# Gathered expert rows in another order: the context's second tile takes two quarters in the first stretch, and x's first mixer starts three pairs later

## The chip, the cores and the metric

The kernel runs on one core of a Trainium2 chip. The metric is the device time of one execution in microseconds, as the median of several runs. TensorE is called PE in the profile, VectorE DVE, ScalarE ACT, GpSimd POOL and SyncE SP.

## What is computed

Two blocks of two layers each, for 256 tokens x and 256 context tokens, width 1024. The part that matters here is the first block. Each of its layers normalises and modulates the tokens, runs a token mixer (a gated linear recurrence with a short convolution), and then an expert layer:

```
qr = (h @ wq)                      # 8 heads, two halves of 128
scores = qr . subkeys              # 128 keys for each half
s1, i1 = top_k(scores[half 0], 16); s2, i2 = top_k(scores[half 1], 16)
top, pos = top_k(s1[:, None] + s2[None, :], 16)
eidx = i1 * 128 + i2 at pos;  gate = softmax(top)
out = sum over 128 chosen e of gate[e] * gelu(u[e] . h) * v[e]
```

Layer 0 does it for the context and for x, layer 1 for x alone. Each token thus takes 128 of 16384 rows of u and v, other rows for every token. The modulation vectors are products of a condition with `w_mod`, 24 MB a layer. The second block (differential attention, a convolution by spectra, two large MLPs) comes after and reads x.

## The kernel before

**Tiles and selections.** 256 tokens are two tiles t of 128 partitions. A selection is one chosen expert of every token of a tile: GpSimd gathers 128 rows of u and v together (8 KB each, 1 MB in all) by one indirect DMA into one of `SLOTS` = 6 buffers `uv` (L2419). VectorE takes the dot product of u with the token (`dot`, L2134), ScalarE the gelu (L1484), VectorE the weight (`weigh`, L2144 or L2146), and v is added by TensorE into a PSUM bank with a diagonal matrix (L1058) or by VectorE into `acc` (L2158). `on_pe` says which: odd selections go to TensorE, except in segments 3 and 6, and all of the first 24. A buffer comes free with its addition, so GpSimd can run six selections ahead.

**Segments and pairs.** `SEGS` lists segments (which, tile, from, to), where which is 0 for the context in layer 0, 1 for x in layer 0, 2 for x in layer 1. The selections of all segments are numbered through; two make a pair g. `PAIRS` holds each segment's last pair: 64, 80, 144, 208, 256, 320, 384. The first weave runs pairs 0 to 256, the second 256 to 384. At a segment's end `flush` (L2161 ff.) adds the sums into the tokens. The context's second tile is split: its first quarter is segment 1, and the other three are segment 4, after the two tiles of x.

**Picks.** A pick (which, tile, quarter) turns the scores of two heads into 32 indices and gates: some 60 VectorE instructions in five pieces (`pick`, L2020 ff., with `top16` at L2002 to L2017). `PICK_ORDER` is their order, `PICK_SLOTS` the pairs at which the five pieces are put in. x's scores use the same memory as the context's, so the context's scores for the later quarters are stored in DRAM (`held`, ScalarE's queue) and read back (`reload_piece`).

**The weave.** Each engine's program is written out by hand with the same function:

```python
for g in range(first, last + 1):
    segment(g, first, last)
    for n, x in enumerate(streams):
        while due[n] is not None and due[n] <= g:
            due[n] = next(x, None)
```

`segment` issues the dots of pair g and the weights and additions of pair g - 1; each stream is a generator that yields the pair at which its next piece is due. The engines run in order and meet at semaphores only. The streams of the first weave are, by pair number: the queries and scores of the context (`WQ[0]`, 0 to 8), four picks (0 to 12), the norm of x (4), its mixer in layer 0 (`TIMES[1]`: eight chunks of `w_in` from 10 on, sixteen scan levels to 34, tail at 35), its output product (`OUT`, 41), norm (`POST`, 46), queries (`WQ[1]`, 52 to 63), eight picks of x (58 to 97), three picks of the context (101 to 115), the modulations of layer 1 and of block two's first layer (`MOD_AT` 84 and 108: 12 chunks of 2 MB each, one every two pairs, TensorE at L833, VectorE's bias at L1730), the convolution filters (`FILTERS`, 136 to 154), and the norm and mixer of x in layer 1 (`TIMES[3]`, from pair 208, `PAIRS[3]`, on; tail at 238 to 240). Pairs 155 to 207 and 241 to 255 have only their gathers.

**Queues.** All weights come through SP in program order into a ring of two 2 MB slots (`ring`); the load of a chunk waits until the chunk two before is used (L589). Gathers come through GpSimd, stores of modulations and `held` through ScalarE.

**After the first weave** a serial part with no gathers follows: the norm of the context (`n_c1`), three chunks of `w_in`, the scan's final states, the output product of x, its norm, queries and first pick. Then the second weave starts, with modulation 3 beside it at pairs 292 to 315.

Of the kernel before, what the change touches and what calls it, by code (L numbers as in the profile page):

```python
# [18 lines left out]
F32 = mybir.dt.float32  # L19
# [4 lines left out]
P = 128  # L24
# [9 lines left out]
PH, PK, TOPK = 8, 128, 16  # L34
NSEL = PH * TOPK
# [36 lines left out]
def program(nc, A, out):  # L72
# [14 lines left out]
    with ctx:  # L87
# [33 lines left out]
        held = nc.dram_tensor("held", [P, 2 * PH - 2 * PH // 4, PK], F32, kind="Internal").ap()  # L121
# [59 lines left out]
        picks = sem("picks")  # L181
# [178 lines left out]
        SEGS = [(0, 0, 0, NSEL), (0, 1, 0, NQ), (1, 0, 0, NSEL), (1, 1, 0, NSEL), (0, 1, NQ, NSEL),  # L360
# [9 lines left out]
        def on_pe(j):  # L370
# [6 lines left out]
        PICK_ORDER = [(0, 0, 0), (0, 1, 0), (0, 0, 1), (0, 0, 2), (0, 0, 3),  # L377
                      (1, 0, 0), (1, 0, 1), (1, 0, 2), (1, 0, 3), (1, 1, 0), (1, 1, 1), (1, 1, 2), (1, 1, 3),
                      (0, 1, 1), (0, 1, 2), (0, 1, 3)]
# [4 lines left out]
        for k, at in zip(PICK_ORDER[1:5], (0, 4, 7, 10)):  # L384
            PICK_SLOTS[k] = [at, at, at + 1, at + 1, at + 2]
        for j, k in enumerate(PICK_ORDER[5:13]):
            PICK_SLOTS[k] = [58 + 5 * j + i for i in range(5)]
        for j, k in enumerate(PICK_ORDER[13:16]):
            PICK_SLOTS[k] = [101 + 5 * j + i for i in range(5)]
# [6 lines left out]
        class Times:  # L396


            def __init__(self, norm, turn, base):
# [10 lines left out]
        TIMES = {1: Times(4, 8, 10), 3: Times(PAIRS[3], PAIRS[3] + 3, PAIRS[3] + 5)}  # L410
        OUT, POST = 41, 46
# [3 lines left out]
              1: [[52 + (4 * c + b) * 3 // 4 for b in range(4)] for c in range(4)]}  # L415
        WQ[2] = [[FIRST_PAIRS + x for x in c] for c in WQ[0]]
        MOD_AT = {1: 84, 2: 108, 3: FIRST_PAIRS + 36}
        FILTERS = 136
# [843 lines left out]
        def _(act):  # L1262
# [154 lines left out]
            def front_pieces(m):  # L1417
                L, times = L_in[m], TIMES[m]
                yield times.evict[0]
                if m == 1:  # L1420
                    act.wait_ge(held_out, 16)
                    act.wait_ge(picks, 5)
                else:
                    act.wait_ge(spec_out, 32)
                for c in range(8):
                    yield times.evict[c]
                    if c < 2:
                        forget(L, c)
                    else:
                        take_chunk(L, c)  # L1430
# [17 lines left out]
            def peer_pieces(p, first):  # L1448
                for c in range(first, 4):
                    yield WQ[p][c][3] + 1  # L1450
                    if c > first:
                        take_score(p, c - 1)
                    query_out(p, c)
                yield WQ[p][3][3] + 3
                take_score(p, 3)
                if p == 0:
                    act.wait_ge(score_out, 8)
                    act.dma_start(held, sc2[1][:, 2 * HQ:, :]).then_inc(held_out, 16)
# [10 lines left out]
            def pick_pieces(keys):  # L1469
                for k in keys:  # L1470
                    yield PICK_SLOTS[k][2]
                    pick_exp(k)

            def reload_piece():
                yield PICK_SLOTS[0, 1, 1][0] - 2
                act.wait_ge(picks, pick_no[0, 1, 1])
                act.dma_start(sc2[1][:, 2 * HQ:, :], held).then_inc(held_in, 16)
# [91 lines left out]
            def early_mods():  # L1569
                for c in range(10, 12):  # L1570
# [14 lines left out]
            weave(0, FIRST_PAIRS, segment, peer_pieces(0, 1), pick_pieces(PICK_ORDER[1:5]),  # L1585
# [3 lines left out]
                  pick_pieces(PICK_ORDER[5:13]), reload_piece(), pick_pieces(PICK_ORDER[13:16]),  # L1589
# [67 lines left out]
        def _(dve):  # L1657
# [362 lines left out]
            def pick(k, slots=None):  # L2020
# [8 lines left out]
                if k == (0, 1, 1):  # L2029
                    dve.wait_ge(held_in, 16)  # L2030
# [173 lines left out]
            def context_pieces():  # L2204
# [16 lines left out]
            weave(0, FIRST_PAIRS, segment, pick_pieces(PICK_ORDER[1:5]), early_mods(),  # L2221
                  norm_pieces("n_x0", xs, TIMES[1].norm), front_pieces(1),
                  itertools.chain(back_pieces(1), norm_pieces("p_x0", xs, POST)),
                  pick_pieces(PICK_ORDER[5:16]),
# [296 lines left out]
```

## Time and profile before

| | us |
|---|---|
| median of 3 runs | 4150.15 |
| lowest and highest | 4144.27, 4165.97 |
| the profiled execution | 4162.62 |
| its span, first to last instruction | 4160.8 |
| first dot of pair 0 | 342.9 |
| last dot of pair 255, and first dot of pair 256 | about 2203, 2401.5 |
| last gather issued | 3268.0 |

The profile is one execution. Its rows are given in microseconds from the span's start; windows can be cut anywhere, and the mean granted TensorE clock stands beside them as a share of full speed. The DMA share is the mean busy share of 16 DMA engines; shares of slightly over one come from packets that are counted where they end. "A <- B" in a row of waits means that the engine and line A sat idle until B had happened.

### The profile page before, as it was taken

To read this page: it belongs to the slowest core of one execution; us is meant where nothing else is said; L and a number is where in the kernel's file an instruction comes from. 1 tells how busy PE (TensorE), PEld (TensorE's weight loads), DVE (VectorE), ACT (ScalarE), POOL (GpSimd) and SP (SyncE) were. 2 spreads that over 40 slices of the span, in tenths; PEclk is the share of its full clock that TensorE was granted. 3 is DMA by queue.
4 is the path that set the end of the run, shared out by engine and by line. 5 is a ranking of instruction groups with operands and counts; after the bars stand their busy time and mean duration, and the time that the engine had idled before them with its cause. 6 is when DMAs were issued, how large, how long until landed. Compare 5 with 4: busy or idle time off the path is not lost.

```text
span 4160.8 us, 30360 instructions
## 1 busy us (share of the span) xinstructions
PE 2609.5 (63%) x10018; PEld 1562.1 (38%) x10018; DVE 2879.5 (69%) x5590; ACT 661.9 (16%) x1096; POOL 927.9 (22%) x794
## 2 busy tenths in 40 slices
PE   7886997765786650007966664666420185987598
PEld 2855574431111110005724441111210163967396
DVE  2646788699885588886876379855889753546354
ACT  1211201111000010001002111000000142533053
POOL 0001233322323333442330022333344200000000
PEclk9998999886898765558967885688665597998899
DMA  7346898987999989998993287898999631445144
GB/s 252 112 152 237 318 363 331 379 327 280 403 393 369 400 323 382 374 372 313 374 369 134 86 314 276 316 370 344 399 377 385 237 125 42 176 156 198 42 167 150
DMA packets 277108, 1156.45 MB, mean 278 GB/s; under 512 B 19128, under 2 KB 19769, under 8 KB 178217
## 3 DMA queue, kind: packets, MB, share of 16 engines
q0 software_dynamic: 112784, 812.45, 50.2%
q1 hardware_dynamic: 162584, 336.37, 22.4%
q10 hardware_dynamic: 1600, 5.96, 0.4%
q8 instruction: 65, 1.06, 0.1%
q14 instruction: 75, 0.61, 0.0%
HBM read 1150.57 MB, written 4.13 MB: 278 GB/s over the span
## 4 chain that ended last, share of the span: by engine, by line
PE 34%; DVE 28%; DMA 28%; issue 9%; ACT 1%; SPq 0%; POOL 0%; POOLq 0%; DVEq 0%; ACTq 0%; PEldq 0%
DMA arena<-in_peer_uv,arena 17%; DMA ring<-in_w_mod 8%; DVE arena L2158 6%; PE ps L725 4%; PE ps L726 4%; PE ps L727 4%; DVE arena L2134 4%; PE ps L1058 4%; PE ps L833 3%; PE ps L951 3%; PE ps L710 2%; PE ps L1014 2%; DVE w_lo L1705 1%; PE ps L819 1%; DVE arena L2008 1%
## 5 line engine op out<-in xcount | busy, mean ns | idle before, releaser
L2419 POOL DMA_INDIRECT arena<-in_peer_uv,arena x768 | 914.0, 1190 | 2348.0 <-DVE arena L2158 1038.6
L1058 PE MATMUL ps<-arena 128*128 128x512 f32 x1072 | 674.6, 764 | 748.7 <-DVE arena L2144 748.4
L2134 DVE CUSTOM_DVE_ANT_0 arena<-arena,hA 128x1024 f32<-128x1024 f32 x512 | 625.9, 1223 | 291.3 <-DMA arena<-in_peer_uv,arena 285.6
L1058 PEld LDWEIGHTS ps<-arena 128*128 128x128 f32 x1072 | 227.5, 232 | 1137.3 <-issue 568.0
L2158 DVE SCALAR_TENSOR_TENSOR arena<-arena 128x1024 f32<-128x1024 f32 x493 | 630.9, 1280 | 0.1
L1484 ACT ACTIVATE arena<-arena 128x2 f32<-128x2 f32 x384 | 78.1, 203 | 2427.9 <-DVE arena L2134 2427.9
L2134 DVE CUSTOM_DVE_ANT_0 arena<-arena,hB 128x1024 f32<-128x1024 f32 x256 | 312.6, 1221 | 113.7 <-DMA arena<-in_peer_uv,arena 111.8
L833 PE MATMUL ps<-ring,condS 128*2 128x512 f32 x576 | 295.4, 661 | 139.7 <-DMA ring<-in_w_mod 139.7
L1705 DVE TENSOR_TENSOR w_lo<-ring,w_hi 128x1024 fp32r<-128x1024 f32 x220 | 264.1, 1222 | 161.3 <-ACT w_hi L1302 154.7
L725 PE MATMUL ps<-hT_hi,w_hi 128*128 128x256 f32 x992 | 287.2, 290 | 28.0 <-DVE hT_lo L1713 25.5
L726 PE MATMUL ps<-hT_lo,w_hi 128*128 128x256 f32 x992 | 285.3, 288 | 0.0
L727 PE MATMUL ps<-hT_hi,w_lo 128*128 128x256 f32 x992 | 285.1, 287 | 0.0
L1302 ACT ACTIVATE w_hi<-ring 128x1024 fp32r<-128x1024 f32 x220 | 231.2, 1060 | 236.3 <-DMA ring<-in_w_mlp_out 88.5
L776 PE MATMUL ps<-ident,hA 128*128 128x128 f32 x128 | 27.5, 404 | 339.0 <-DVE hA L1755 330.5
L725 PEld LDWEIGHTS ps<-hT_hi,w_hi 128*128 128x128 f32 x992 | 195.5, 197 | 30.3 <-issue 27.2
L951 PE MATMUL ps<-hT,ring 128*128 128x256 f32 x896 | 201.0, 379 | 0.8 <-ACT hT L1332 0.8
L726 PEld LDWEIGHTS ps<-hT_lo,w_hi 128*128 128x128 f32 x992 | 195.4, 197 | 0.0
L727 PEld LDWEIGHTS ps<-hT_hi,w_lo 128*128 128x128 f32 x992 | 195.2, 197 | 0.0
L833 PEld LDWEIGHTS ps<-ring,condS 128*2 128x2 f32 x576 | 46.2, 90 | 380.1 <-issue 223.4
L951 PEld LDWEIGHTS ps<-hT,ring 128*128 128x128 f32 x896 | 170.3, 190 | 44.1 <-issue 20.1
L1014 PE MATMUL ps<-hT,ring 128*128 128x256 f32 x768 | 175.2, 386 | 1.4 <-ACT hT L1309 1.4
L1014 PEld LDWEIGHTS ps<-hT,ring 128*128 128x128 f32 x768 | 148.7, 194 | 33.3 <-issue 11.6
(292 smaller groups left out, 3401.0 us busy)
## 6 DMA issues: line engine op xcount, KB each, us to landing
ring<-in_w_mod SPq DMA_DIRECT2D x48, 2048.0 KB
ring<-in_w_in SPq DMA_DIRECT2D x16, 2048.0 KB
ring<-in_w_mlp_in SPq DMA_DIRECT2D x64, 512.0 KB, 6.3
ring<-in_w_mlp_out SPq DMA_DIRECT2D x64, 512.0 KB, 5.8
ring<-in_peer_wq SPq DMA_DIRECT2D x12, 2048.0 KB
ring<-in_w_in SPq DMA_DIRECT2D x44, 512.0 KB, 5.9
vec<-mods SPq DMA_DIRECT2D x31, 512.0 KB
ring<-in_w_out SPq DMA_DIRECT2D x6, 2048.0 KB
```

Source lines behind the costliest of these rows:

```text
L725: pe.matmul(out_, stationary[0], moving[0], start=first, stop=False)
L726: pe.matmul(out_, stationary[0], moving[1], start=False, stop=False)
L727: return pe.matmul(out_, stationary[1], moving[0], start=False, stop=last)
L833: mm = pe.matmul(o, condS[:, k, 2 * (l // 2):2 * (l // 2) + 2], ring[:, s, k, :], start=k == 0, stop=k == KT - 1)
L951: mm = pe.matmul(o, ring[:, s, k, b * P:(b + 1) * P], hT[:, k, :], start=k == 0, stop=k == KT - 1)
L1014: mm = pe.matmul(o, ring[:, s, k, b * P:(b + 1) * P], hT[:, k, :], start=k == 0, stop=k == KT - 1)
L1058: mm = pe.matmul(ps[:, 6 + c, :], uv[:, j % SLOTS, 0:P], uv[:, j % SLOTS, D + c * CW:D + (c + 1) * CW], start=start, stop=stop)
L1302: act.activation(w_hi[:, s, ks, :], ring[:, s, ks, :], ACT.Copy).then_inc(high_done, 1)
L1705: dve.tensor_tensor(w_lo[:, s, ks, :], ring[:, s, ks, :], w_hi[:, s, ks, :].bitcast(F32), ALU.subtract).then_inc(low_done, 1)
L2134: dve.tensor_tensor_reduce(row, row, peer_buf[p][:, t, :], 1.0, 0.0, ALU.mult, ALU.add, dots[:, column(j):column(j) + 1]).then_inc(dot_don ...
L2158: ins = dve.scalar_tensor_tensor(acc, row, c, acc, ALU.mult, ALU.add)
L2419: pool.indirect_dma_start(uv[:, j % SLOTS, :], None, A["peer_uv"], at).then_inc(uv_full[j % SLOTS], 16)
```

## The change

Segment 1 takes two quarters (64 selections, 32 pairs) of the context's second tile, and segment 4 the other two. `PAIRS` becomes 64, 96, 160, 224, 256, 320, 384. Pick (0, 1, 1) moves from slots 101 to 105 to slots 13 to 15. The first mixer of x, its output, norm, queries and the picks behind it start three pairs later; the modulations and filters start twelve pairs later; the mixer of x in layer 1 starts at `PAIRS[3]`, sixteen pairs later, and so ends at 256. `held` keeps half of the second tile's scores instead of three quarters.

```diff
--- before.py
+++ after.py
@@ -118,7 +118,7 @@
         hid_lo = rounded("hid_lo", [P, FF // P, T], "arena", FF // P * T)
         ps = ctx.enter_context(nc.psum_tensor("ps", [P, 8, 512], F32))
         spectra = nc.dram_tensor("spectra", [2, T, D], F32, kind="Internal").ap()
-        held = nc.dram_tensor("held", [P, 2 * PH - 2 * PH // 4, PK], F32, kind="Internal").ap()
+        held = nc.dram_tensor("held", [P, PH, PK], F32, kind="Internal").ap()
         mods = nc.dram_tensor("mods", [4, 2, 6 * D], F32, kind="Internal").ap()
 
         class Area:
@@ -357,7 +357,7 @@
         HQ, NQ = PH // PARTS, NSEL // PARTS
 
 
-        SEGS = [(0, 0, 0, NSEL), (0, 1, 0, NQ), (1, 0, 0, NSEL), (1, 1, 0, NSEL), (0, 1, NQ, NSEL),
+        SEGS = [(0, 0, 0, NSEL), (0, 1, 0, 2 * NQ), (1, 0, 0, NSEL), (1, 1, 0, NSEL), (0, 1, 2 * NQ, NSEL),
                 (2, 0, 0, NSEL), (2, 1, 0, NSEL)]
         PEER_GATE = [mod(0, C, 5), mod(0, X, 5), mod(0, C, 5), mod(1, X, 5)]
         GATE_OF = [0, 0, 1, 1, 2, 3, 3]
@@ -374,19 +374,19 @@
         dve_upto = [j - n for j, n in enumerate(pe_upto)]
 
 
-        PICK_ORDER = [(0, 0, 0), (0, 1, 0), (0, 0, 1), (0, 0, 2), (0, 0, 3),
+        PICK_ORDER = [(0, 0, 0), (0, 1, 0), (0, 0, 1), (0, 0, 2), (0, 0, 3), (0, 1, 1),
                       (1, 0, 0), (1, 0, 1), (1, 0, 2), (1, 0, 3), (1, 1, 0), (1, 1, 1), (1, 1, 2), (1, 1, 3),
-                      (0, 1, 1), (0, 1, 2), (0, 1, 3)]
+                      (0, 1, 2), (0, 1, 3)]
         PICK_ORDER += [(2, t, q) for t in range(NT) for q in range(PARTS)]
         pick_no = {k: j for j, k in enumerate(PICK_ORDER)}
 
         PICK_SLOTS = {}
-        for k, at in zip(PICK_ORDER[1:5], (0, 4, 7, 10)):
+        for k, at in zip(PICK_ORDER[1:6], (0, 4, 7, 10, 13)):
             PICK_SLOTS[k] = [at, at, at + 1, at + 1, at + 2]
-        for j, k in enumerate(PICK_ORDER[5:13]):
-            PICK_SLOTS[k] = [58 + 5 * j + i for i in range(5)]
-        for j, k in enumerate(PICK_ORDER[13:16]):
-            PICK_SLOTS[k] = [101 + 5 * j + i for i in range(5)]
+        for j, k in enumerate(PICK_ORDER[6:14]):
+            PICK_SLOTS[k] = [61 + 5 * j + i for i in range(5)]
+        for j, k in enumerate(PICK_ORDER[14:16]):
+            PICK_SLOTS[k] = [104 + 5 * j + i for i in range(5)]
         for k, at in zip(PICK_ORDER[17:20], (4, 7, 10)):
             PICK_SLOTS[k] = [FIRST_PAIRS + at + i // 2 for i in range(5)]
         for j, k in enumerate(PICK_ORDER[20:]):
@@ -407,15 +407,15 @@
                 self.level = [r + 4 + i for i in range(16)]
                 self.tail = r + 21
 
-        TIMES = {1: Times(4, 8, 10), 3: Times(PAIRS[3], PAIRS[3] + 3, PAIRS[3] + 5)}
-        OUT, POST = 41, 46
+        TIMES = {1: Times(4, 8, 13), 3: Times(PAIRS[3], PAIRS[3] + 3, PAIRS[3] + 5)}
+        OUT, POST = 44, 49
 
 
         WQ = {0: [[], [0, 0, 1, 1], [2, 2, 3, 3], [4, 4, 5, 5]],
-              1: [[52 + (4 * c + b) * 3 // 4 for b in range(4)] for c in range(4)]}
+              1: [[55 + (4 * c + b) * 3 // 4 for b in range(4)] for c in range(4)]}
         WQ[2] = [[FIRST_PAIRS + x for x in c] for c in WQ[0]]
-        MOD_AT = {1: 84, 2: 108, 3: FIRST_PAIRS + 36}
-        FILTERS = 136
+        MOD_AT = {1: 96, 2: 120, 3: FIRST_PAIRS + 36}
+        FILTERS = 148
         KV = FIRST_PAIRS + 66
 
 
@@ -1419,7 +1419,7 @@
                 yield times.evict[0]
                 if m == 1:
                     act.wait_ge(held_out, 16)
-                    act.wait_ge(picks, 5)
+                    act.wait_ge(picks, 6)
                 else:
                     act.wait_ge(spec_out, 32)
                 for c in range(8):
@@ -1455,7 +1455,7 @@
                 take_score(p, 3)
                 if p == 0:
                     act.wait_ge(score_out, 8)
-                    act.dma_start(held, sc2[1][:, 2 * HQ:, :]).then_inc(held_out, 16)
+                    act.dma_start(held, sc2[1][:, 4 * HQ:, :]).then_inc(held_out, 16)
 
             def peer_start(p):
                 query_out(p, 0)
@@ -1472,9 +1472,9 @@
                     pick_exp(k)
 
             def reload_piece():
-                yield PICK_SLOTS[0, 1, 1][0] - 2
-                act.wait_ge(picks, pick_no[0, 1, 1])
-                act.dma_start(sc2[1][:, 2 * HQ:, :], held).then_inc(held_in, 16)
+                yield PICK_SLOTS[0, 1, 2][0] - 2
+                act.wait_ge(picks, pick_no[0, 1, 2])
+                act.dma_start(sc2[1][:, 4 * HQ:, :], held).then_inc(held_in, 16)
 
             def segment(g, first, last):
 
@@ -1582,11 +1582,11 @@
             turn_norm("p_c0")
             peer_start(0)
             pick_exp((0, 0, 0))
-            weave(0, FIRST_PAIRS, segment, peer_pieces(0, 1), pick_pieces(PICK_ORDER[1:5]),
+            weave(0, FIRST_PAIRS, segment, peer_pieces(0, 1), pick_pieces(PICK_ORDER[1:6]),
                   itertools.chain(early_mods(), gate_piece(0, 12), gate_piece(1, PAIRS[1] + 2), gate_piece(2, PAIRS[3] + 2)),
                   norm_pieces("n_x0", TIMES[1].norm, TIMES[1].turn), front_pieces(1), back_pieces(1),
                   itertools.chain(norm_pieces("p_x0", POST), peer_pieces(1, 0)),
-                  pick_pieces(PICK_ORDER[5:13]), reload_piece(), pick_pieces(PICK_ORDER[13:16]),
+                  pick_pieces(PICK_ORDER[6:14]), reload_piece(), pick_pieces(PICK_ORDER[14:16]),
                   itertools.chain(modulation(1), modulation(2), filter_pieces(), norm_pieces("n_x1", TIMES[3].norm)),
                   front_pieces(3))
             root(0)
@@ -2026,7 +2026,7 @@
                 yield next(slots)
                 h = slice(q * HQ, (q + 1) * HQ)
                 r = slice(q * NQ, (q + 1) * NQ)
-                if k == (0, 1, 1):
+                if k == (0, 1, 2):
                     dve.wait_ge(held_in, 16)
                 if p != 0 or t == 0 or q == 0:
                     dve.wait_ge(score_out, 8 * p + 2 * q + t + 1)
@@ -2218,10 +2218,10 @@
             mixer0()
             norm("p_c0", cs)
             run(pick((0, 0, 0)))
-            weave(0, FIRST_PAIRS, segment, pick_pieces(PICK_ORDER[1:5]), early_mods(),
+            weave(0, FIRST_PAIRS, segment, pick_pieces(PICK_ORDER[1:6]), early_mods(),
                   norm_pieces("n_x0", xs, TIMES[1].norm), front_pieces(1),
                   itertools.chain(back_pieces(1), norm_pieces("p_x0", xs, POST)),
-                  pick_pieces(PICK_ORDER[5:16]),
+                  pick_pieces(PICK_ORDER[6:16]),
                   itertools.chain(modulation(1), modulation(2), filter_pieces(), norm_pieces("n_x1", xs, TIMES[3].norm)),
                   front_pieces(3))
             norm("n_c1", cs)
```

## Rows read from the trace of the kernel before

**Rows 1.** The page: span, busy time (share) and instructions of each engine.

```profile
span 4160.8 us, 30360 instructions
...
PE 2609.5 (63%) x10018; PEld 1562.1 (38%) x10018; DVE 2879.5 (69%) x5590; ACT 661.9 (16%) x1096; POOL 927.9 (22%) x794
```

**Rows 2.** The page: the chain that ended last, by engine and by line.

```profile
PE 34%; DVE 28%; DMA 28%; issue 9%; ACT 1%; SPq 0%; POOL 0%; POOLq 0%; DVEq 0%; ACTq 0%; PEldq 0%
DMA arena<-in_peer_uv,arena 17%; DMA ring<-in_w_mod 8%; DVE arena L2158 6%; PE ps L725 4%; PE ps L726 4%; PE ps L727 4%; DVE arena L2134 4%; PE ps L1058 4%; PE ps L833 3%; PE ps L951 3%; PE ps L710 2%; PE ps L1014 2%; DVE w_lo L1705 1%; PE ps L819 1%; DVE arena L2008 1%
```

**Rows 3.** Windows: us, busy by engine (records), PEclk, DMA share, GB/s.

```profile
422.10:450.70 28.60, 20.96 (x50) 7.88 (x51) 24.95 (x86) 4.38 (x8) 5.26 (x5) 0.82 0.72 282
450.70:481.40 30.70, 30.22 (x110) 17.66 (x109) 25.21 (x87) 5.46 (x10) 5.75 (x6) 1.00 0.85 318
821.90:1021.80 199.90, 117.28 (x290) 58.72 (x289) 191.33 (x556) 25.89 (x52) 58.03 (x53) 0.72 0.82 312
1021.80:1127.10 105.30, 84.67 (x166) 18.79 (x167) 100.16 (x273) 11.23 (x23) 32.72 (x28) 0.87 0.97 378
1127.10:1155.80 28.70, 15.34 (x30) 3.33 (x28) 13.21 (x24) 0.61 (x3) 6.11 (x5) 0.76 0.92 362
1155.80:1233.80 78.00, 61.52 (x128) 13.65 (x127) 73.51 (x211) 7.62 (x16) 25.64 (x21) 0.93 1.02 406
1233.80:1272.90 39.10, 30.16 (x59) 6.86 (x58) 36.53 (x106) 3.81 (x8) 10.65 (x11) 0.83 1.00 389
1272.90:1386.70 113.80, 76.44 (x154) 16.87 (x152) 59.91 (x106) 2.84 (x14) 38.05 (x28) 0.87 0.96 381
1386.70:1415.30 28.60, 22.67 (x44) 4.67 (x44) 8.53 (x16) 0.41 (x2) 6.18 (x5) 0.81 1.04 368
1574.50:1865.90 291.40, 0.00 (x0) 0.00 (x0) 260.27 (x417) 10.59 (x52) 123.68 (x104) 0.50 0.98 374
1865.90:2114.50 248.60, 211.83 (x892) 149.96 (x892) 194.91 (x351) 28.69 (x55) 72.94 (x65) 0.91 0.91 349
2114.50:2206.00 91.50, 54.30 (x65) 17.02 (x66) 65.04 (x116) 4.54 (x17) 31.44 (x29) 0.65 0.92 342
2206.00:2401.50 195.50, 119.38 (x536) 91.19 (x534) 88.75 (x167) 34.70 (x39) 4.46 (x5) 0.79 0.26 93
2702.00:2870.60 168.60, 113.23 (x224) 24.83 (x222) 85.47 (x151) 4.07 (x20) 51.73 (x39) 0.84 0.94 372
```

**Rows 4.** Windows of L2134 alone: us, busy (records), PEclk, DMA share, GB/s.

```profile
821.90:1021.80 199.90, 63.88 (x105) 0.72 0.82 312
1233.80:1272.90 39.10, 12.23 (x21) 0.83 1.00 389
1272.90:1386.70 113.80, 34.48 (x57) 0.87 0.96 381
2114.50:2206.00 91.50, 39.36 (x64) 0.65 0.92 342
```

**Rows 5.** Waits of VectorE, pairs 116 to 129: total us, times, longest.

```profile
DVE arena L2134 <- DMA arena<-in_peer_uv,arena: 36.4, 25, 4.2
DVE mod_io L1730 <- PE ps L833: 19.2, 3, 10.6
```

**Rows 6.** Timeline: the last addition of the flush at pair 256.

```profile
2210.34 1.23 DVE L2182 TENSOR_TENSOR cs<-cs,arena 128x1024 f32<-128x1024 f32 x1
```

**Rows 7.** Waits of all engines, pairs 10 to 19: total us, times, longest.

```profile
POOL arena L2419 <- PE ps L1058: 70.3, 14, 15.1
...
DVE arena L2134 <- DMA arena<-in_peer_uv,arena: 27.5, 13, 5.9
```

## The prediction

> **What bounds the kernel now.** I read the page first. VectorE is the busiest engine, 2879.5 us of a span of 4160.8, and no engine is near full [rows 1]. The chain that ended last gives the gathers of the expert rows its largest single share, 17%, and the modulation weights (`w_mod`) 8%; VectorE's accumulation and dot products, L2158 and L2134, have 6% and 4% [rows 2]. So inside the gather stretches two resources take turns, the 16 DMA engines and VectorE, and a mean over the span says nothing of what a shift is worth. I therefore cut the first 256 pairs of gathered rows into windows whose bounds are starts of a pair's first dot product [rows 3]; a dot leaves two records on L2134, so a pair leaves four, and the records give the number of pairs (105 for the 26 pairs 58 to 83) [rows 4]. The reader should compare time per pair, VectorE busy per pair and the DMA share:
> - nothing beside the gathers: 291.4 us for 52 pairs, 5.6 each, DMA share 0.98, VectorE 5.0 busy. Pairs 240 to 255, the part that goes: 91.5 us for 16, 5.7 each, VectorE busy 65.0, share 0.92. DMA bound.
> - picks without weights (58 to 83): 199.9 us, 7.7 each, VectorE 191.3 of it, DMA share 0.82. VectorE bound.
> - picks and modulation weights together (84 to 97): 105.3 us, 7.5 each; (101 to 110): 78.0, 7.8 each, DMA share 1.02 and 406 GB/s. Both at once: a 2 MB chunk every two pairs costs there next to nothing over a pick alone.
> - modulation weights alone (116 to 129): 113.8 us, 8.1 each, VectorE busy 4.3. VectorE stands idle 36.4 us for gathered rows and 19.2 us behind the bias addition at L1730 [rows 5].
> - x's second mixer (208 to 239): 248.6 us, 7.8 each.
>
> **The change part by part.** 256 pairs before and after; only what runs beside each changes. Pairs 0 to 9 keep their work.
>
> *One pick more at the start.* Pick (0, 1, 1) gets slots 13 to 15 and x's first mixer starts at 13 instead of 10, so pairs 10 to 12 carry a pick without mixer chunks, and 13 to 15 do what 10 to 12 did, with the next pick. The nearest row is pairs 7 to 9, a pick in three pairs: 28.6 us, VectorE busy 24.95 [rows 3]. There both rows of a pair are added by TensorE; from pair 12 on one is VectorE's, 1.28 us instead of a diagonal of about 0.3, so 24.95 + some 2 = 27. Pairs 10 to 12 took 30.7 with chunks: upper bound 31. Lower bound: the pick hides wholly in idle time and three pairs cost 3 x 5.6 = 17. I take **+27**, because VectorE was busy 25.2 of the 30.7 us and can't hide a pick there.
>
> *Three later.* Everything from the mixer's chunks to the second last context pick moves with it: pairs 16 to 113 are pairs 13 to 110. Transfers moved with them: the `w_in` and `w_out` chunks, the gate row, `wq`. SP's order is unchanged and each load waits for a ring slot, not for a pair number; POOL waits for picks, which are farther ahead of use (the first pick of x ends at 65 and is first used at 96; before 62 and 80). Pairs 87 to 95 lose the modulation chunks they ran beside, but are VectorE bound with them (105.3 us with 100.2 busy) and without (7.7 a pair): **0**. `held` shrinks from 12 to 8 of 16 rows of scores, 786 to 524 KB each way, under a microsecond of DMA and covered.
>
> *Modulation weights twelve later.* 24 chunks over 48 pairs, now 96 to 143, while picks end at 113. Before, 29 of these 48 pairs had a pick; now 15. From pair 114 on: pairs 111 to 115 (pick and chunks, 39.1 us) have no counterpart, and 16 pairs of chunks alone (113.8 + 28.6) become 30. 14 more at 113.8 / 14 = 8.13: +113.8 - 39.1 = +74.7. At the rate of the last modulation, 168.6 us for 20 pairs, 8.43 each [rows 3], it is +79. The other bound is by bytes: the 48 pairs and their chunks took 105.3 + 28.7 + 78.0 + 39.1 + 113.8 + 28.6 = 393.5 us at DMA shares of 0.92 to 1.04; if they take the same again, what is added is nine pairs of picks without chunks, 9 x 7.5: +67. I take **+71**, the middle, since the low DMA share of 0.96 in the pick-free pairs says that some is lost, but not that all of it is.
> The Trainium skill (DMA: Bandwidth & Descriptors, Issuing engines are not separate DMA queues) says that transfers of scalar, sync and gpsimd end on the same 16 DMA engines and interleave. By that rule the window is its bytes and the term is the lower one, the sum four microseconds less. The trace agrees where picks stand beside chunks (share 1.02) and less so where they don't (0.96).
>
> *Pure gather pairs.* Filters (now 148), and the empty stretch up to the last context stretch: 80 pairs (144 to 223) for 76: **+22** (4 x 5.6). The filter stage stands partly in a segment where TensorE adds; at most 2 us less, left in the range.
>
> *The last context stretch.* 32 pairs instead of 48. The mixer of x for layer 1 keeps its 32 pairs and price, 248.6 us; pairs 240 to 255 go: **-91.5**. Its convolution ends now at the stretch's last place, so one gate multiplication of 128x1024 stands between the last flush and the context's norm: **+1.2**, as the flush's last addition [rows 6]. The serial part behind (195.5 us) needs two chunks of `w_in`; the second is requested when chunk 7 is done, three pairs and some 14 us of flush and norm before its use, so 0, at worst one chunk's time.
>
> Sum: 27 + 71 + 22 - 91.5 + 1.2 = **+30**. In words: the removed pairs were cheap (5.7 us), because a pair that only gathers costs what its bytes cost; the pairs that come instead stand at work that fills another engine, and three picks' worth of VectorE work loses its cover. Against the profiled execution (4162.6 us, span 4160.8) this is 4193; the runs' median is 4150.15, 12.5 lower, and 4150.15 + 30 = **4180**, 0.7% slower. 0.5%, 21 us, is about what a measurement of this kernel can tell from no change.
>
> **The rivals.**
> *A, the pick hides.* In pairs 10 to 19 VectorE waits 27.5 us for gathered rows [rows 7]; if that takes up ten of the pick's microseconds, the first term is 17 and the sum +20: 4170. For it: that idle time. Against: it lies mostly behind pair 12, where the mixer's chunks hold TensorE, and that pattern is only moved.
> *B, the start itself becomes faster (not slower in all).* The gathers of pairs 10 to 19 are issued late since POOL waits 70.3 us for TensorE's additions, which stand behind the mixer's matmuls [rows 7]. Three pairs without chunks let POOL fill the six slots; if the 27.5 us and the 8 us of other waits there all vanish, the sum is 30 - 36 = -6: 4144, no change. It decides when over 9 us of them go, and makes the kernel faster only past 51. Against: six slots are three pairs of lead, used up in three pairs; the matmuls stay.
> *C, more is lost at the seams.* The pick-free chunks run at 8.43 (+8 over 71) and the second `w_in` chunk is late by some 8 us at the stretch's end: +46, 4196. For it: TensorE's clock is granted at 0.72 to 0.93 in these windows, and pairs 7 to 9 lie before a mixer that starts at 1.00 [rows 3]; a quieter start could cost it that.
> *D, it isn't what bounds.* If single bytes decided everywhere, the sum of bytes is unchanged and so is the time: 4150. Against: in 58 to 83 the DMA share is 0.82.
>
> **How the numbers follow.** Forecast 0.60, A 0.10, B 0.10, C 0.13, D 0.07. Slower by over 0.5%: forecast and C less the forecast's low edge, 0.71. Within: A, most of B and D, 0.22. Faster: the ends of B and D, 0.07. The terms' own bounds give 17 + 67 + 20 - 91.5 + 0 = +12 to 31 + 79 + 24 - 91.5 + 9 = +52; with A and C inside, and the scatter of the three runs (4144 to 4166) on top, the range is 4156 to 4206.
>
> **What would show it.** In the changed kernel's windows: pair 256 starts some 30 us later; pairs 0 to 15 take about 27 us more than pairs 0 to 12 did; pairs 87 to 95 stand at 7.5 with a DMA share near 0.8; pairs 114 to 143 at 8.1 to 8.4 with VectorE half idle; pairs 224 to 255 as 208 to 239 did; VectorE's busy total is unchanged, its waits for gathered rows longer. The forecast is wrong if chunks alone cost under 7 us a pair, if the mixer's pairs 13 to 22 run clearly faster than 10 to 19, or if the serial part changes by over 5 us.

## The result, and the profile after

The changed kernel takes 4178.84 us (median of 5 runs, 4171.62 to 4183.75) against 4155.62 for the kernel before (5 runs): 1.0066 times as long, 95% interval 1.0049 to 1.0084. By the medians that is +23 us where +30 was forecast; the interval reaches from +20 to +35. The profiled execution took 4178.84 us, 16.2 more than the one of before.

The page's first lines and its chain say little more than those of before: VectorE is busy as long as it was, 1.3 us more, and the span is 16.3 us longer. In the chain the share of the modulation weights has grown from 8 to 9%, and that of the gathers has shrunk from 17 to 15%.

```profile
span 4177.1 us, 30365 instructions
...
PE 2602.1 (62%) x10018; PEld 1559.6 (37%) x10018; DVE 2880.8 (69%) x5590; ACT 663.9 (16%) x1096; POOL 929.3 (22%) x794
...
DMA arena<-in_peer_uv,arena 15%; DMA ring<-in_w_mod 9%; DVE arena L2158 6%; PE ps L725 4%; PE ps L726 4%; PE ps L727 4%; PE ps L1058 4%; PE ps L833 4%; DVE arena L2134 4%; PE ps L951 3%; PE ps L1014 2%; PE ps L710 2%; DVE w_lo L1705 1%; PE ps L819 1%; DMA vec<-mods 1%
```

The windows tell where the time went. They are the changed kernel's, cut at first dots of pairs 0, 10, 13, 16, 61, 87, 96, 144, 156, 168, 224, 255 and 256, and the last one holds pairs 292 to 319, whose program did not change. Columns as in [rows 3]; a DMA packet counts whole in the window in which it starts, so a share can pass one.

```profile
346.80:454.20 107.40, 81.73 (x291) 51.45 (x292) 85.20 (x271) 19.41 (x31) 19.16 (x18) 0.86 0.73 281
454.20:484.50 30.30, 23.87 (x59) 9.33 (x58) 25.13 (x87) 5.47 (x10) 6.47 (x6) 0.86 0.88 322
484.50:512.80 28.30, 24.07 (x79) 16.65 (x79) 27.12 (x89) 3.41 (x6) 7.46 (x7) 0.85 0.72 269
512.80:847.70 334.90, 290.58 (x1115) 192.27 (x1114) 258.09 (x450) 36.95 (x73) 109.25 (x90) 0.92 0.93 358
847.70:1042.10 194.40, 115.72 (x297) 58.83 (x295) 188.45 (x553) 25.96 (x52) 57.20 (x53) 0.75 0.86 323
1042.10:1105.00 62.90, 32.64 (x36) 10.21 (x36) 61.35 (x165) 7.44 (x15) 20.31 (x17) 0.58 0.76 275
1105.00:1497.20 392.20, 282.28 (x560) 62.61 (x560) 253.86 (x563) 18.25 (x57) 120.03 (x96) 0.86 0.96 378
1497.20:1579.40 82.20, 49.77 (x73) 14.19 (x71) 51.46 (x96) 10.12 (x21) 29.99 (x24) 0.69 1.01 394
1579.40:1674.70 95.30, 45.92 (x68) 16.54 (x68) 70.30 (x107) 9.10 (x17) 27.80 (x25) 0.64 0.76 292
1674.70:1993.00 318.30, 0.00 (x0) 0.00 (x0) 279.62 (x448) 11.51 (x56) 132.95 (x112) 0.50 0.97 368
1993.00:2228.40 235.40, 204.16 (x888) 148.16 (x888) 188.48 (x336) 28.57 (x54) 70.39 (x61) 0.92 0.94 360
2228.40:2432.20 203.80, 122.18 (x540) 91.23 (x540) 98.25 (x185) 36.12 (x41) 4.47 (x5) 0.78 0.26 90
2709.50:2924.00 214.50, 154.88 (x304) 35.76 (x304) 118.41 (x209) 5.75 (x28) 70.10 (x56) 0.86 0.98 383
```

For the comparison some windows of the kernel before are needed that [rows 3] doesn't have: pairs 13 to 57, 132 to 143, 144 to 155, 208 to 254, 255 with the serial part, and 292 to 319.

```profile
481.40:821.90 340.50, 295.49 (x1138) 196.60 (x1137) 257.64 (x449) 36.84 (x73) 108.36 (x92) 0.92 0.93 357
1415.30:1486.90 71.60, 41.84 (x52) 13.00 (x52) 51.45 (x96) 9.53 (x20) 30.65 (x23) 0.61 1.01 407
1486.90:1574.50 87.60, 38.26 (x55) 13.88 (x54) 74.24 (x111) 9.63 (x18) 28.02 (x24) 0.60 0.82 314
1865.90:2200.40 334.50, 262.49 (x952) 165.81 (x952) 254.64 (x456) 31.74 (x70) 104.38 (x93) 0.84 0.92 353
2200.40:2401.50 201.10, 123.02 (x540) 92.37 (x540) 94.07 (x176) 36.18 (x41) 4.46 (x5) 0.79 0.26 92
2677.90:2905.80 227.90, 155.95 (x304) 35.50 (x304) 118.24 (x209) 5.69 (x28) 70.84 (x56) 0.84 0.91 357
```

Stretch by stretch, after less before:

| what | before | after | us |
|---|---|---|---|
| pairs 10 to 12; 10 to 15 after | 30.7 | 58.6 | +27.9 |
| mixer of x to its queries, 45 pairs | 340.5 | 334.9 | -5.6 |
| picks, then picks and chunks, to the last chunk; 74 and 83 pairs | 593.4 | 649.5 | +56.1 |
| filters and gathers alone; 76 and 80 pairs | 450.6 | 495.8 | +45.2 |
| last context stretch to pair 254; 47 and 31 pairs | 334.5 | 235.4 | -99.1 |
| pair 255 and the serial part | 201.1 | 203.8 | +2.7 |

With -0.4 for pairs 0 to 9, pair 256 starts 26.8 us later after pair 0 than it did. Pair 0 itself starts 3.9 later, and 14.4 us come back behind pair 256, where nothing changed, 13.4 of them in pairs 292 to 319 alone (214.5 for 227.9). That is scatter: the profiled execution of before had a slow last modulation (the same 28 pairs took 213.6 to 223.0 us in the changed kernel and in the kernels e1 to e8 below). So the stretch that changed shows +27 in these two profiles, the medians +23, and the two profiled executions +16. One profile of each kernel doesn't settle the sizes: in a second profile of the changed kernel (e5) the same stretch, pair 0 to pair 256, took 2062.0 us instead of 2085.4, with the same program. The table that sets two profiles of each kernel side by side stands in the part on why the prediction was right.

### The profile page after: what moved, and what is told of

Its sections match the earlier page's. It is cut to its first block, busy times and chain, and to the rows that moved or that the text cites. A ratio compares the mean times of both kernels' runs of the same rounds, so it can differ in the third digit from the quotient of the medians.

```text
span 4177.1 us, 30365 instructions
## 1 busy us (share of the span) xinstructions
PE 2602.1 (62%) x10018; PEld 1559.6 (37%) x10018; DVE 2880.8 (69%) x5590; ACT 663.9 (16%) x1096; POOL 929.3 (22%) x794
## 4 chain that ended last, share of the span: by engine, by line
PE 35%; DVE 28%; DMA 27%; issue 8%; ACT 1%; SPq 0%; POOL 0%; POOLq 0%; DVEq 0%; PEldq 0%
DMA arena<-in_peer_uv,arena 15%; DMA ring<-in_w_mod 9%; DVE arena L2158 6%; PE ps L725 4%; PE ps L726 4%; PE ps L727 4%; PE ps L1058 4%; PE ps L833 4%; DVE arena L2134 4%; PE ps L951 3%; PE ps L1014 2%; PE ps L710 2%; DVE w_lo L1705 1%; PE ps L819 1%; DMA vec<-mods 1%
## 5 line engine op out<-in xcount | busy, mean ns | idle before, releaser
L2134 DVE CUSTOM_DVE_ANT_0 arena<-arena,hA 128x1024 f32<-128x1024 f32 x512 | 626.2, 1223 | 249.0 <-DMA arena<-in_peer_uv,arena 242.9
L2134 DVE CUSTOM_DVE_ANT_0 arena<-arena,hB 128x1024 f32<-128x1024 f32 x256 | 312.9, 1222 | 160.6 <-DMA arena<-in_peer_uv,arena 159.3
L725 PE MATMUL ps<-hT_hi,w_hi 128*128 128x256 f32 x992 | 286.4, 289 | 28.2 <-DVE hT_lo L1713 25.7
L727 PEld LDWEIGHTS ps<-hT_hi,w_lo 128*128 128x128 f32 x992 | 194.4, 196 | 0.0
```

What stands on the lines that cost most here:

```text
L725: pe.matmul(out_, stationary[0], moving[0], start=first, stop=False)
L727: return pe.matmul(out_, stationary[1], moving[0], start=False, stop=last)
L2134: dve.tensor_tensor_reduce(row, row, peer_buf[p][:, t, :], 1.0, 0.0, ALU.mult, ALU.add, dots[:, column(j):column(j) + 1]).then_inc(dot_don ...
```

## The experiments

The theory to be tested, called the cover theory in the expectations, is that of the prediction: a gather pair beside a pick is bound by VectorE and leaves the DMA engines a fifth to a quarter idle, a pair beside modulation chunks is bound by its bytes, and the kernel pays for every picked pair that has no chunks. Its rivals put the cost at the start (the mixer begins later and a pick more stands ahead of it) or at the segments. Each kernel was timed together with fresh runs of the kernel before; differences in us are differences of these medians, and the brackets give the 95% interval of the ratio. The first four kernels cut the change into steps: e1 and e2 lead from the kernel before to e3, which the modulations and filters alone separate from the changed kernel; e4 is that one part by itself.

**e1, everything three later.** x's first mixer, its output, norm, queries and the picks behind it start three pairs later, as in the change, and so do the modulations (87 and 111) and the filters (139). No pick moves from its place in the order, and x's second mixer stays at 208.

```diff
-            PICK_SLOTS[k] = [58 + 5 * j + i for i in range(5)]
+            PICK_SLOTS[k] = [61 + 5 * j + i for i in range(5)]
...
-            PICK_SLOTS[k] = [101 + 5 * j + i for i in range(5)]
+            PICK_SLOTS[k] = [104 + 5 * j + i for i in range(5)]
...
-        TIMES = {1: Times(4, 8, 10), 3: Times(PAIRS[3], PAIRS[3] + 3, PAIRS[3] + 5)}
-        OUT, POST = 41, 46
+        TIMES = {1: Times(4, 8, 13), 3: Times(PAIRS[3], PAIRS[3] + 3, PAIRS[3] + 5)}
+        OUT, POST = 44, 49
...
-        MOD_AT = {1: 84, 2: 108, 3: FIRST_PAIRS + 36}
-        FILTERS = 136
+        MOD_AT = {1: 87, 2: 111, 3: FIRST_PAIRS + 36}
+        FILTERS = 139
```

> The kernel before with x's first mixer, its output, norm, queries, the picks behind it, the modulations (87 and 111) and the filters (139) three pairs later; no pick moved, segments as before. Cover theory (a shift costs only where VectorE work loses the transfers it ran beside): three chunk pairs without the fourth pick instead of three pure gather pairs behind the filters, +3 us against before, between -3 and +6. Start theory (the whole cost of the change is at its start, because the mixer begins later): +15 or more. Segment theory: 0.

4146.13 us against 4153.12 of before, 0.9990 [0.9969, 1.0012]: no change. A later mixer alone costs nothing that shows; the interval excludes more than 5 us.

**e2, the pick early.** e1 with the change's pick order and slots (61 and 104 on), `picks` 6 and `held` halved; segments as before. Two places of the edit against e1:

```diff
+        for k, at in zip(PICK_ORDER[1:6], (0, 4, 7, 10, 13)):
...
+        for j, k in enumerate(PICK_ORDER[14:16]):
+            PICK_SLOTS[k] = [104 + 5 * j + i for i in range(5)]
```

> As e1, and pick (0, 1, 1) in slots 13 to 15 instead of 104 to 108, held halved; segments still as before (one quarter in segment 1, three in segment 4). Cover theory: the pick leaves the pairs with modulation chunks, where it was free (those pairs are bound by their bytes), and costs 6 to 10 us at the start: +11 against before. Start theory: +28 or more, the whole of the change. Segment theory: still near 0.

4159.33 us, 1.0025 [1.0004, 1.0046], so 13 us over e1 (0.35% by the ratios). Two windows of each kernel, pairs 13 to 15 and the 48 pairs with chunks (87 to 134), of e1:

```profile
484.70:503.80 19.10, 19.10 (x73) 13.91 (x73) 11.41 (x22) 0.61 (x3) 6.76 (x7) 0.96 0.97 370
1039.50:1424.30 384.80, 278.63 (x559) 61.87 (x560) 292.03 (x731) 26.53 (x66) 121.15 (x95) 0.86 0.97 381
```

and of e2:

```profile
478.10:506.20 28.10, 24.05 (x83) 16.31 (x82) 27.11 (x88) 3.41 (x6) 7.71 (x7) 0.90 0.71 262
1036.80:1425.20 388.40, 287.60 (x576) 63.59 (x576) 276.32 (x663) 23.73 (x63) 119.35 (x96) 0.87 0.97 380
```

The pick adds 15.7 us of VectorE work and 9.0 us of time to pairs 13 to 15. Taken out of the pairs with chunks it saves nothing there: VectorE does 15.7 us less in them, and they last 3.6 us longer (which is within the scatter of such a window, 13 us between two executions of one program, as e9 shows below). The two profiled executions as wholes lie the other way round (e1 4158.89, e2 4147.86), so the pick's cost in all rests on the medians, and only its cost in its own pairs on these rows.

**e3, the segments.** The changed kernel with the modulations and filters nine pairs back.

```diff
-        MOD_AT = {1: 96, 2: 120, 3: FIRST_PAIRS + 36}
-        FILTERS = 148
+        MOD_AT = {1: 87, 2: 111, 3: FIRST_PAIRS + 36}
+        FILTERS = 139
```

> The changed kernel with the modulations at 87 and 111 and the filters at 139, so three later than before instead of twelve; segments 64 and 64. Differs from e2 in the segments alone, and from the changed kernel in the modulations and filters alone. Cover theory: the segments alone are worth 0 to 3 us (pure gather pairs cost the same wherever they stand), so +11 against before, and 12 to 20 us below the changed kernel. Start theory: equal to the changed kernel, +23 to +28. Segment theory (what costs is x's second mixer against the end of the stretch, or two quarters in segment 1): equal to the changed kernel, and over e2 by 15 or more.

4161.63 us, 1.0019 [1.0002, 1.0037]. It can't be told from e2 (1.0025), which differs from it in the segments alone: two quarters in segment 1, and x's second mixer against the end of the stretch, are worth nothing that shows (the 15 us or more that the segment theory wants over e2 would have). The segment theory falls. The changed kernel, timed in other sessions, was 1.0066 and 1.0054 (e5) of the same kernel before, so what is left, 0.35 to 0.47% or 15 to 20 us, belongs to the nine pairs by which modulations and filters moved beyond the rest.

**e4, the modulations and filters alone.**

```diff
-        MOD_AT = {1: 84, 2: 108, 3: FIRST_PAIRS + 36}
-        FILTERS = 136
+        MOD_AT = {1: 96, 2: 120, 3: FIRST_PAIRS + 36}
+        FILTERS = 148
```

> The kernel before with only the modulations (96 and 120 instead of 84 and 108) and the filters (148 instead of 136) twelve pairs later. Cover theory: pairs 84 to 95 keep their picks at 7.5 us without chunks, the 48 pairs with chunks stay bound by their bytes at some 393 us, and twelve pure pairs of 5.6 us are gone: 12 x 1.9 = +23 us against before, as much as the whole change. Start and segment theories: 0.

4184.34 us, 1.0072 [1.0048, 1.0096], +31 us, where +23 was expected: this one part, alone, costs at least as much as the whole change (the interval starts at +20). Its windows, pairs 84 to 95 (picks without chunks now) and 96 to 143 (the chunks):

```profile
1024.50:1112.50 88.00, 41.31 (x48) 12.84 (x48) 85.87 (x245) 10.83 (x21) 25.71 (x24) 0.62 0.77 285
1112.50:1508.70 396.20, 288.16 (x576) 63.88 (x576) 253.33 (x570) 18.14 (x57) 120.76 (x97) 0.86 0.96 376
```

The twelve pairs take 7.3 us each with the DMA engines 0.77 busy and VectorE busy 85.9 of 88.0. The 48 pairs behind them carry 39 us less of VectorE work than before (253.3 for 291.9) and take 396.2 for 393.5. The start theory, by which the whole cost lies at the start, falls too; what does lie there is the pick's share, as e2 shows.

**e5, the changed kernel again.**

> The changed kernel once more, beside the three that follow. +20 to +28 us against before by every theory; it gives the scatter of windows that are the same program, above all the last modulation's pairs 292 to 319.

4176.55 us, 1.0054 [1.0034, 1.0075], +25 us. The profiled execution, 4164.24, was 12 us faster than the median. Its windows of pairs 96 to 143, 156 to 167 (filters) and 168 to 223 (gathers alone):

```profile
1108.10:1503.20 395.10, 286.75 (x577) 63.85 (x576) 254.15 (x564) 18.14 (x57) 120.55 (x97) 0.87 0.97 382
1577.60:1670.80 93.20, 41.89 (x68) 15.40 (x68) 70.06 (x108) 9.07 (x17) 26.98 (x23) 0.69 0.78 293
1670.80:1973.90 303.10, 0.00 (x0) 0.00 (x0) 280.09 (x449) 11.41 (x56) 138.26 (x112) 0.50 0.99 389
```

The same 56 pairs of gathers took 303.1 us here and 318.3 in the other profile of this kernel, 389 and 368 GB/s: 15 us of scatter in work that only moves bytes.

**e6, the filters in the segment of VectorE.** One surprise of the result was the filter stage. Its VectorE waited 12.0 us for the product of the taps (L1153), before 5.6, in the changed kernel:

```profile
DVE arena L2107 <- PE ps L1153: 12.0, 2, 8.7
```

and in the one before:

```profile
DVE arena L2107 <- PE ps L1153: 5.6, 2, 3.2
```

The two products of the taps are now due at pairs 158 and 159, the last of segment 2, and stand there on TensorE behind additions of expert rows, which wait for VectorE's weights. (`PAIRS` gives the first pair of the next segment: segment 3 begins at 160.) e6 puts the stage into segment 3, whose rows VectorE adds alone.

```diff
-        FILTERS = 148
+        FILTERS = 162
```

> The changed kernel with the filters at 162 instead of 148, so that their taps stand wholly in the segment that VectorE adds alone (160 to 223). If the 7.7 us that pairs 156 to 167 took over pairs 144 to 155 of before come from the round trip (VectorE waits for the taps' product at L1153, which stands on TensorE behind the addition that waits for VectorE's weight), they go: 6 to 10 us below the changed kernel. If they are scatter of the gathers: 0.

4183.31 us, 1.0064 [1.0041, 1.0087], beside 1.0054 for e5: nothing gained. Pairs 156 to 181 take 72.7 + 96.4 = 169.1 us in e6, 168.4 in e5 and 174.8 in the changed kernel's first profile. (e6 has the whole filter stage in them, the other two only its part from 156 on, which is 3.3 us less of VectorE work.) The two parts in e6, cut at pairs 156, 168 and 182:

```profile
1579.50:1652.20 72.70, 18.65 (x24) 5.71 (x24) 60.76 (x105) 6.33 (x17) 27.47 (x25) 0.57 0.93 355
1652.20:1748.60 96.40, 31.81 (x50) 11.98 (x50) 82.32 (x127) 12.91 (x23) 31.59 (x27) 0.59 0.86 321
```

The wait itself went, from 12.0 us (10.8 in e5) to 5.1:

```profile
DVE arena L2107 <- PE ps L1153: 5.1, 2, 2.6
```

So the round trip was there and moving the stage removed it, but that saved no time that the runs show. The expectation of 6 to 10 us was wrong: a shorter wait of VectorE was not a shorter kernel.

**e7, the other way.** The cover theory says not only what a later modulation costs but what an earlier one gives.

```diff
-        MOD_AT = {1: 84, 2: 108, 3: FIRST_PAIRS + 36}
+        MOD_AT = {1: 68, 2: 92, 3: FIRST_PAIRS + 36}
```

> The kernel before with only the modulations sixteen pairs earlier, at 68 and 92, so that they stand beside picks from 68 on (45 of 48 pairs). Cover theory, from the other side: pairs 68 to 83 turn from 7.6 us without chunks into chunk pairs, and sixteen pairs of 5.6 are won for them: 16 x 1.9 = -30 us against before, between -20 and -35, and a kernel faster than both. If the chunks instead meet an engine that is full (VectorE at 7.3 of 7.6 us, so each wait for a chunk is lost time): 0 or slower.

4128.29 us against 4151.78, 0.9948 [0.9926, 0.9970], -23 us: faster than both kernels. Pairs 58 to 67, 68 to 115 (chunks) and 116 to 131 take 571.1 us together, where the kernel before took 593.4:

```profile
822.70:900.50 77.80, 57.40 (x225) 39.74 (x223) 73.66 (x207) 14.26 (x27) 21.94 (x20) 0.91 0.92 353
900.50:1290.10 389.60, 293.03 (x572) 65.39 (x572) 346.06 (x966) 34.93 (x75) 115.85 (x96) 0.85 0.98 381
1290.10:1393.80 103.70, 54.07 (x70) 16.14 (x68) 64.29 (x114) 3.25 (x16) 41.62 (x32) 0.69 1.02 395
```

The 48 pairs with chunks now hold 346 us of VectorE work instead of the changed kernel's 254, and take 389.6 instead of 392.2 us. The gain is at the low end of what I expected (-20 to -35). What SP loads behind the last chunk (the filter tables, the rows of the next norm and two chunks of `w_in`) was not free in its new place either: pairs 116 to 131 took 6.5 us each, at a DMA share of 1.02, where gathers alone take 5.6. Counted to pair 207, behind those loads, the profiles show 29 us (1015.0 for 1044.0), about the 30 expected; but e7's profiled execution was 13 us faster than its median.

**e8, the same on the changed kernel.** Modulations at 71 and 95, filters at 162.

> The changed kernel with the modulations at 71 and 95 (25 pairs earlier) and the filters at 162. Cover theory: 25 pairs of picks get their chunks back (-47 at 1.9 us each) and the filters' 8 us go: -25 to -30 us against before. It should lie within 8 us of e7, on the slow side by the pick's price at the start. If the chunks find VectorE full: near before.

4137.32 us, 0.9961 [0.9940, 0.9981]. The change's loss of 23 us has become a gain of 14, at most 25 by the interval; I had expected 25 to 30, and no run shows what took the rest. It lies 9 us behind e7 by the medians (5 by the ratios), where up to 8 was foretold.

**e9, a place that the change doesn't touch.** The last modulation of the kernel before stands behind the picks of the second weave too.

```diff
-        MOD_AT = {1: 84, 2: 108, 3: FIRST_PAIRS + 36}
+        MOD_AT = {1: 84, 2: 108, 3: FIRST_PAIRS + 10}
```

> The kernel before with only the third modulation (block two's last layer, in the second weave) 26 pairs earlier, at pair 266 instead of 292, beside the picks of x in layer 1 (265 to 288, 7.3 us a pair without chunks). A place the change does not touch. Cover theory: 22 picked pairs take the chunks and 22 pairs of 5.6 us stand in for them: 22 x 1.7 = -37 us against before, between -25 and -42. If the cost of the change was something of its own place (x's chunks, the mixer, the segments): 0 here.

4117.23 us against 4156.63, 0.9910 [0.9880, 0.9940]: -39 us. Pairs 266 to 289, 290 to 315 and 316 to 341 of the kernel before:

```profile
2489.00:2666.10 177.10, 83.71 (x97) 26.10 (x96) 172.19 (x504) 18.86 (x39) 54.21 (x48) 0.61 0.75 281
2666.10:2870.60 204.50, 140.62 (x278) 31.64 (x276) 109.70 (x194) 5.29 (x26) 67.35 (x53) 0.85 0.95 373
2870.60:3044.20 173.60, 92.93 (x192) 37.62 (x192) 137.03 (x218) 12.83 (x36) 64.62 (x52) 0.72 0.94 374
```

and of e9:

```profile
2491.30:2683.70 192.40, 137.93 (x269) 30.69 (x268) 179.17 (x515) 18.86 (x39) 59.46 (x48) 0.86 0.94 366
2683.70:2854.00 170.30, 95.64 (x124) 28.78 (x124) 103.07 (x183) 5.28 (x26) 62.25 (x52) 0.68 0.92 357
2854.00:3012.30 158.30, 83.94 (x173) 35.98 (x172) 135.80 (x216) 12.85 (x36) 62.77 (x52) 0.73 0.96 376
```

The picked pairs take the chunks for 15.3 us more, DMA share 0.75 to 0.94, and the pairs left without them cost 34.2 less. Another 15.3 us lie in the next 26 pairs, where the loads of the next weights (`in_attn_w_qkv`) no longer follow a late chunk: the first is issued at 2707 us instead of 2890. The profile of before was slow there, though. In the nine other profiles with the same program in these pairs (the changed kernel and e1 to e8), the 26 pairs took 164.8 to 167.4 us, and the three windows together 540.4 to 549.1 instead of 555.2. Against those, e9's 521.0 is a gain of 19 to 28 us, not 34. The medians say 39, with an interval from 25 to 50.

**e10, all three earlier.** e7 and e9 together.

> The kernel before with all three modulations earlier: 68 and 92 as in e7, and 266 as in e9. Cover theory: the two gains are at different places and add: -22 (e7 as measured) - 37 = -59 us against before, a kernel faster than both.

4089.83 us, 0.9848 [0.9821, 0.9874], -67 us against before and about 90 below the changed kernel. The two gains add: -23 and -39 are -62, well inside the interval (-52 to -74).

## Why the prediction was right, point by point

**How far the terms can be read.** Each of the two kernels has a second profile of its first 256 pairs: e5 is the changed kernel again, and e9 has the kernel before's program up to there. Rows of e9, for all 256 pairs and for pairs 58 to 83, 84 to 131 (chunks), 132 to 143, 156 to 207 (gathers alone) and 208 to 254:

```profile
344.80:2403.40 2058.60, 1271.79 (x3998) 671.78 (x3998) 1586.07 (x3343) 211.88 (x433) 595.98 (x513) 0.78 0.86 329
823.90:1023.70 199.80, 112.97 (x291) 57.79 (x289) 191.25 (x556) 25.89 (x52) 59.57 (x53) 0.74 0.83 313
1023.70:1404.00 380.30, 280.30 (x556) 62.28 (x556) 291.74 (x729) 26.53 (x66) 113.93 (x95) 0.86 0.98 386
1404.00:1489.40 85.40, 53.88 (x74) 15.29 (x74) 51.45 (x96) 9.99 (x21) 32.12 (x25) 0.63 1.02 396
1576.50:1872.00 295.50, 0.00 (x0) 0.00 (x0) 259.98 (x417) 10.60 (x52) 121.89 (x104) 0.50 0.98 369
1872.00:2202.70 330.70, 257.15 (x952) 164.46 (x952) 254.86 (x458) 31.73 (x70) 105.27 (x93) 0.86 0.94 356
```

and of e5, for all 256 pairs and for pairs 61 to 95 and 144 to 155:

```profile
347.10:2409.10 2062.00, 1264.36 (x3998) 670.65 (x3998) 1587.54 (x3343) 211.77 (x433) 607.81 (x513) 0.79 0.85 328
850.50:1107.90 257.40, 148.11 (x334) 69.33 (x332) 249.88 (x718) 33.32 (x67) 78.00 (x70) 0.71 0.84 312
1502.90:1577.30 74.40, 42.80 (x54) 13.34 (x54) 51.36 (x96) 10.08 (x21) 30.13 (x24) 0.63 1.01 405
```

| what | before, e9 | changed, e5 | difference, by choice of profiles | forecast |
|---|---|---|---|---|
| pairs 10 to 12; 10 to 15 after | 30.7, 31.1 | 58.6, 58.9 | +27.5 to +28.2 | +27 |
| mixer of x to its queries | 340.5, 339.9 | 334.9, 336.9 | -3.0 to -5.6 | 0 |
| picks, chunks and twelve pairs behind them | 665.0, 665.5 | 731.7, 726.8 | +61.3 to +66.7 | +71 |
| filter pairs (144 to 155; 156 to 167 after) | 87.6, 87.1 | 95.3, 93.2 | +5.6 to +8.2 | 0 to -2 |
| gathers alone, 52 and 56 pairs | 291.4, 295.5 | 318.3, 303.1 | +7.6 to +26.9 | +22 |
| last context stretch to pair 254 | 334.5, 330.7 | 235.4, 231.6 | -95.3 to -102.9 | -91.5 |
| pair 255 and the serial part | 201.1, 200.7 | 203.8, 203.8 | +2.7 to +3.1 | +1.2 |
| pair 0 to pair 256 | 2058.6, 2058.6 | 2085.4, 2062.0 | +3.4 to +26.8 | +30 |

The total that counts is therefore the medians' (+23, and +25 in e5), not a profile's.

- **The direction and its cause** held. The kernel became slower because picks and modulation chunks were pulled apart; e4 shows it by itself, e7, e9 and e10 show it from the other side. The forecast was +30, the medians show +23. VectorE's total was unchanged, as said; its waits for gathered rows were to grow and did not visibly (397.4 us before, 402.2 after, 380.7 in e5).
- **The pick at the start**, +27: 58.6 for 30.7 is +27.9. What a pick in idle time would have cost (rival A, 17) did not come. The step mixes two things that e1 and e2 part: three pairs more at the start (19.1 us in e1), which e1 shows to be free in the sum since three go elsewhere, and the pick, 9.0 us in its pairs for 15.7 us of VectorE work.
- **Everything three later**, 0: -5.6 over 45 pairs (from 13 on before, from 16 on after). The gain lies in the first seven of them. They took 65.1 to 66.3 us in the five kernels whose mixer starts at 10 (before, e4, e7, e9, e10), 62.8 in e1, and 59.6 to 61.1 in the six with the early pick; the other 38 took 273 to 277 in all twelve. This is a small piece of rival B. SP requests the first chunk of `w_in` at pair 10 in both kernels (at 450.1 us before and 453.5 after), so with the mixer at 13 its first loads are done before their use, and with the pick in pairs 13 to 15 the DMA share there is only 0.72; which of the two gives how much was not separated. By the prediction's own sign, pairs 13 to 22 took 89.4 us where 10 to 19 took 96.3: faster by 7, so 0 was not right here, but it is short of the 9 us at which B would have decided and far from its 36.
- **The modulations twelve later**, +71 between bounds of 67 and 79: this term was somewhat too large. In the first two profiles it measures +56.1, but the edge of that window is not a clean cut. What SP loads behind the last chunk falls partly before it and partly behind it, and that differs between executions of one program: the 48 pairs with chunks took 393.5 us in before and 380.3 in e9, and the twelve pairs behind them 71.6 and 85.4. With these twelve pairs counted in, the term is +61.3 to +66.7. Two steps of it were off: pairs 87 to 95 ran at 7.0 us each, not 7.5, and pairs 61 to 86 took 194.4 us where 58 to 83 took 199.9, with segment 1's flush gone from pair 80 into the pairs with chunks.
- **The bytes decided** in the pairs with chunks, as the prediction's lower bound had it. In all twelve profiles these 48 pairs moved bytes at 376 to 386 GB/s, with anything from 253 to 346 us of VectorE work in them; they took 380.3 to 398.1 us for 146 to 151 MB (rate times time). The longest is e8's:

```profile
920.50:1318.60 398.10, 291.57 (x577) 64.98 (x576) 330.75 (x899) 32.12 (x72) 116.28 (x97) 0.87 0.98 380
```

  The Trainium skill (DMA: Bandwidth & Descriptors, Issuing engines are not separate DMA queues) says that transfers of all issuing engines run on the same 16 DMA engines and interleave. By that rule the lower term was to be taken, and here these windows agree with it. Within pairs 114 to 141 of the changed kernel VectorE still waited 42.0 us behind the bias addition, at a DMA share of 0.97: the engines moved bytes meanwhile.

```profile
DVE mod_io L1730 <- PE ps L833: 42.0, 7, 12.7
```

- **Filters and gathers alone**, +22: +45.2 in the first two profiles. Of it 10.6 (82.2 for 71.6) belong to the term above. The filter pairs, which I had put at up to 2 us less, cost 5.6 to 8.2 more in every choice of profiles, and e6 says that their longer wait at L1153 is not what makes the kernel longer; the cause stays open. The four pairs more that only gather are +26.9 in one choice and +7.6 in another around the 22 that were forecast: scatter.
- **The last context stretch**, -91.5 and +1.2: -99.1 and +2.7, the serial part under its sign of 5. The stretch is 4 to 11 us shorter than the forecast made it, since its 31 pairs with the mixer ran faster too (235.4 and 231.6 us, where 208 to 238 took 241.7 and 238.4). e3 shows that its place costs nothing that can be seen.
- **Rivals C and D** fell. Nothing more was lost at the seams: the chunks without picks ran at 8.1 us a pair (pairs 114 to 143), not 8.43, and the second mixer's pairs ran faster, not slower. The granted clock was lower at the start (0.86 in pairs 10 to 12 for 1.00, 0.85 in 13 to 15), but pairs 10 to 12 took 30.3 us for 30.7, and the 45 mixer pairs have 0.92 in both. D: the time did change with an unchanged sum of bytes, since the DMA share of picked pairs without chunks was 0.76 after as it was 0.82 before.

So the direction, the mechanism and the two large terms (pairs lost and won) were right. That the sum came so close is in part luck: in the first two profiles the terms miss by -15 (modulations), +23 (filters and gathers), -6 (last stretch with the serial part) and -6 (three later), and these cancel to -3. Some 11 us of each of the first two are loads that stand on the other side of a window's edge, and about 5 of the second are scatter; the mis-sized terms that stay in every choice are the modulations' (61 to 67 for 71), the filter pairs' (+6 to +8 for 0 to -2), the mixer's (-3 to -6 for 0) and the last stretch's (4 to 11 us more saved).

## What to carry to other kernels

Where a stream is bound now by an engine and now by its bytes, put the other transfers beside the engine-bound part, and judge a move of work by what it stands beside before and after, not by how many steps move. The cheapest stretches are not the ones to shorten: pairs at 5.7 us with nothing beside them were saved here and pairs at 7 us with idle DMA engines were bought. A kernel's own profile shows such places as windows where one engine is full and the DMA share is 0.75 to 0.85, next to windows where it is 1.0; moving three load streams by their start numbers alone gave 1.5% (e10). And before a term of a sum is judged by a window, the same window of a second execution should be at hand: here they differed by up to 15 us.

## What was not expected of the hardware

The gathers alone ran at 368 GB/s in one execution and 389 in another of the same program, over 300 us each; a difference of 15 us between two profiles of this kernel needs no other cause. Why they differ is not shown. Twelve chunks of 2 MB beside gathers (pairs 292 to 319) took 227.9 and 214.5 us in the kernel before and the changed one, whose program is the same there. Gathers of 8 KB rows and 2 MB loads together reached 406 GB/s over 78 us [rows 3], more than the gathers alone.
